# A hybrid decoder step on one core: the last channel mixer's router and row work move ahead of its norm

## The reference

```
def rms_norm(x, g):
    y = x * rsqrt(mean(x * x, axis=-1) + EPS)
    return y * g

hn = rms_norm(h, norm_ffn_g[1])            # the norm this change is about
logits = hn @ router_w                     # 1024 -> 8
top_v, top_i = top_k(logits, 2)
gates = softmax(top_v)
for e in range(8):
    out += combine[:, e] * ((silu(hn @ w_gate[e]) * (hn @ w_up[e])) @ w_down[e])
y = rms_norm(h + out, final_norm_g)
```

## Time and profile before

| what | us |
|---|---|
| median of the runs | 1647.79 |
| the profiled execution | 1648.3 |
| its span, from the first to the last instruction | 1646.6 |
| last product of w_out ends | 819.96 |
| first product of the experts starts | 854.24 |
| PE busy over the span | 1566.2 (95%) |
| mean granted clock of PE | 0.971 |

### The profile page before, as it was taken

The page is one execution under the profiler, slowest core; times in us unless marked ns, Lnnn a source line. Parts: engine busy times, 40 slices in busy tenths (PEclk is TensorE's granted clock), DMA queues, the critical chain, the costliest instruction groups (busy, mean ns, idle before and its releaser), DMA issues.

```text
span 1646.6 us, 25254 instructions
## 1 busy us (share of the span) xinstructions
PE 1566.2 (95%) x8782; PEld 1387.3 (84%) x8783; DVE 1173.3 (71%) x1497; ACT 1000.4 (61%) x1184; POOL 110.6 (7%) x112
## 2 busy tenths in 40 slices
PE   6989999999999998999969999999999999999993
PEld 5889999899999878999858888888888888888882
DVE  6677437544444477734738989898998989898894
ACT  5663324443433575233437787878888787887772
POOL 3020120000000002111000000000000000010000
PEclk9999999999999999999979999999999999999997
DMA  7434453455445332444449999999999999999994
GB/s 221 133 118 128 136 154 117 127 152 145 146 142 159 116 116 93 136 140 128 141 135 352 359 373 372 374 375 366 374 369 372 379 373 369 368 377 366 373 367 155
DMA packets 223037, 399.08 MB, mean 242 GB/s; under 512 B 12336, under 2 KB 103520, under 8 KB 222960
## 3 DMA queue, kind: packets, MB, share of 16 engines
q1 hardware_dynamic: 215920, 372.84, 64.9%
q0 software_dynamic: 6544, 23.37, 5.2%
q10 hardware_dynamic: 496, 1.84, 0.3%
HBM read 383.84 MB, written 14.16 MB: 242 GB/s over the span
## 4 chain that ended last, share of the span: by engine, by line
PE 72%; DVE 9%; ACT 6%; DMA 6%; issue 6%; ACTq 0%; SPq 0%; DVEq 0%; POOLq 0%; POOL 0%
PE bank L1462 10%; PE bank L1464 10%; PE bank L1463 10%; PE bank L1774 7%; PE bank L1776 7%; PE bank L1775 6%; PE bank L1766 4%; PE bank L1765 4%; PE bank L1767 4%; DMA weights_raw<-in_moe_w_up 3%; DVE weights_low L1348 3%; DMA weights_raw<-in_moe_w_down 2%; PE bank L1608 2%; ACT weights_high L909 2%; ACT weights_high L689 2%
## 5 line engine op out<-in xcount | busy, mean ns | idle before, releaser
L1348 DVE TENSOR_TENSOR weights_low<-weights_raw,weights_high 128x1024 fp32r<-128x1024 f32 x522 | 621.4, 1220 | 76.6 <-ACT weights_high L909 65.3
L909 ACT ACTIVATE weights_high<-weights_raw 128x1024 fp32r<-128x1024 f32 x522 | 548.8, 1060 | 144.4 <-DMA weights_raw<-in_moe_w_up 56.4
L972 DVE TENSOR_TENSOR weights_low<-weights_raw,weights_high 128x1024 fp32r<-128x1024 f32 (+1 forms) x186 | 225.2, 1216 | 297.4 <-ACT weights_high L689 297.3
L689 ACT ACTIVATE weights_high<-weights_raw 128x1024 fp32r<-128x1024 f32 (+1 forms) x186 | 193.4, 1045 | 246.6 <-PE bank L1464 236.3
L1462 PE MATMUL bank<-moving_high,weights_high 128*128 128x320 f32 x944 | 299.7, 317 | 1.0 <-DVE moving_low L1043 1.0
L1463 PE MATMUL bank<-moving_low,weights_high 128*128 128x320 f32 x944 | 295.5, 313 | 0.0
L1464 PE MATMUL bank<-moving_high,weights_low 128*128 128x320 f32 x944 | 295.4, 313 | 0.0
L1774 PE MATMUL bank<-weights_high,expert_in_high 128*128 128x512 f32 (+1 forms) x768 | 290.6, 378 | 1.7 <-DVE weights_low L1348 0.8
L1776 PE MATMUL bank<-weights_high,expert_in_low 128*128 128x512 f32 (+1 forms) x768 | 286.6, 373 | 0.0
L1775 PE MATMUL bank<-weights_low,expert_in_high 128*128 128x512 f32 (+1 forms) x768 | 286.4, 373 | 0.0
L1462 PEld LDWEIGHTS bank<-moving_high,weights_high 128*128 128x128 f32 x944 | 181.3, 192 | 4.6 <-issue 1.9
(11 more groups left out here) (298 smaller groups left out, 1813.9 us busy)
## 6 DMA issues: line engine op xcount, KB each, us to landing
weights_raw<-in_moe_w_gate SPq DMA_DIRECT2D x176, 512.0 KB, 5.5
weights_raw<-in_moe_w_up SPq DMA_DIRECT2D x176, 512.0 KB, 5.7
weights_raw<-in_moe_w_down SPq DMA_DIRECT2D x176, 512.0 KB, 5.3
weights_raw<-in_w_in SPq DMA_DIRECT2D x80, 512.0 KB, 3.6
weights_raw<-in_dense_w_gate SPq DMA_DIRECT2D x22, 512.0 KB, 3.8
weights_raw<-in_dense_w_up SPq DMA_DIRECT2D x22, 512.0 KB, 3.7
weights_raw<-in_w_out SPq DMA_DIRECT2D x16, 512.0 KB, 3.4
weights_raw<-in_dense_w_down SPq DMA_DIRECT2D x16, 512.0 KB, 3.4
```

The source lines that it names most:

```text
L689: fn(whi[:, p % RING, 0:n], raw[:, p % RING, 0:n], ACT.Copy).then_inc(high_done, 1)
L909: fn(whi[:, p % RING, 0:n], raw[:, p % RING, 0:n], ACT.Copy).then_inc(high_done, 1)
L1348: v.tensor_tensor(wlo[:, p % RING, 0:n], raw[:, p % RING, 0:n], whi[:, p % RING, 0:n].bitcast(F), ALU.subtract).then_inc(low_done, 1)
```

## The change

Four things. First, the last norm's eight tiles become h times gain, without the inverse root, and are made by DVE right behind each residual tile (line 1092 of the changed kernel). Router products and the turning to rows work on these tiles, most of them between the chunks of w_out; the two best logits of a token are the same with or without a positive factor. Second, the inverse root enters at the difference of the two best logits before Exp, as a third column beside row number and gate, and, by slot, as the scale of Silu and as a factor of the product with up. Third, the squares' sum, the root, the residual's rows and the first expert's gates come behind the first expert's row numbers, and the second half of the rows goes to memory by a shorter write. Fourth, ranks and counts are fewer products, and pick is one instruction for three.

The core of the diff:

```diff
+        HALF = D // 2
+        pool.wait_ge(y_ready, NT)
+        pool.dma_start(HN[0:TP, 0:HALF].rearrange("(t p) d -> p t d", p=128), hn[:, 0:PAIRS, 0:HALF]).then_inc(hn_first, 16)
+        pool.dma_start(HN[TP:T, 0:HALF], hn[0:64, PAIRS, 0:HALF]).then_inc(hn_first, 16)
+        pool.dma_start(HN[T:T + CAP, 0:HALF], hn[:, 0, 0:HALF]).then_inc(hn_first, 16)
+        pool.dma_start(HN[T:T + CAP, HALF:D], hn[:, 0, 0:HALF]).then_inc(hn_first, 16)
+        pool.wait_ge(hn_first, 64)
+        pool.wait_ge(hn_out, 32)
+        pool.wait_ge(idx_ready, 1)
+        pool.indirect_dma_start(out=xrow[:], out_offset=None, in_=HN,
+                                in_offset=bass.IndirectOffsetOnAxis(ap=idx[:, 0:1], axis=0)).then_inc(xrow_in, 16)
...
+        def normed_rows(hf_):
+
+            for t, (_, sz) in enumerate(TOK):
+                act.wait_ge(hn_psum, NT * hf_ + t + 1)
+                fn(hn[0:sz, t, 512 * hf_:512 * hf_ + 512], bank[4 + t][0:sz, :], ACT.Copy).then_inc(y_ready, 1)
...
+                    if L == LAST and part == 3:
+                        act.wait_ge(pstate_out, 16 * LAYERS)
+                        act.wait_ge(vrow_out, 16 * LAYERS)
+                        for q in s0_out:
+                            act.wait_ge(q, 16 * LAYERS)
+                        normed_rows(0)
...
+        normed_rows(1)
+        act.wait_ge(y_ready, NO)
+        act.dma_start(HN[0:TP, 512:D].rearrange("(t p) d -> p t d", p=128), hn[:, 0:PAIRS, 512:D]).then_inc(hn_out, 16)
+        act.dma_start(HN[TP:T, 512:D], hn[0:64, PAIRS, 512:D]).then_inc(hn_out, 16)
+        split_high(NDENSE + AHEAD - 1, 1)
+        act.wait_ge(stat_psum, 2 * LAYERS)
+        fn(rcol[:], bank[2][:, 0:NT], ACT.Sqrt, bias=eps_t[:], scale=1.0 / D).then_inc(root_ready, 1)
+        nc.scalar.preload_act_table(ACT.Exp)
...
-        fn(g1[:, 0], g1[:, 0], ACT.Exp).then_inc(gap_top, 1)
+        fn(g1[:, 1], g1[:, 1], ACT.Exp).then_inc(gap_top, 1)
...
-                fn(sge[:, j % 2, 0:cols], bank[2 * (j % 2)][:, 0:cols], ACT.Silu).then_inc(gate_emptied, 1)
+                if j == 0:
+                    act.wait_ge(rnow_ready, item + 1)
+                fn(sge[:, j % 2, 0:cols], bank[2 * (j % 2)][:, 0:cols], ACT.Silu, scale=rnow[:, 0:1]).then_inc(
+                    gate_emptied, 1)
...
+                        if L == LAST:
+                            dve.wait_ge(dve_emptied, tile[(L, sec, j)][3])
+                            v.tensor_scalar(xn[:, j, :], h[:, j, :], prm[:, P_FFN + KD * L + j:P_FFN + KD * L + j + 1],
+                                            None, ALU.mult).then_inc(xn_ready, 1)
...
+        add_square(2 * LAYERS - 1, KD - 2)
+        add_square(2 * LAYERS - 1, KD - 1)
...
+        v.tensor_tensor(slot[:], bank[0][:, 0:NT * NE].rearrange("p (t e) -> p t e", e=NE), mk[:], ALU.mult).then_inc(
+            shift_done, 1)
...
+        def gates():
+
+            split_low(NDENSE + AHEAD - 1, 1)
+            dve.wait_ge(root_ready, 2 * LAYERS)
+            link(v.tensor_tensor(g1[:, 0], top[:, :, 1], top[:, :, 0], ALU.subtract))
+            link(v.reciprocal(rcol[:], rcol[:]))
+            v.tensor_tensor(g1[:, 1], g1[:, 0], rcol[:], ALU.mult).then_inc(top_ready, 1)
+            v.tensor_copy(pair[:, :, 2:3], rcol[:].unsqueeze(2))
+            dve.wait_ge(count_psum, 1)
+            v.tensor_copy(fullf[:, 0, 0:NE], bank[1][:, 0:NE]).then_inc(count_read, 1)
+            dve.wait_ge(gap_top, 1)
+            link(v.tensor_scalar(g1[:, 0], g1[:, 1], 1.0, None, ALU.add))
+            link(v.reciprocal(g1[:, 2], g1[:, 0]))
+            link(v.tensor_tensor(g1[:, 3], g1[:, 1], g1[:, 2], ALU.mult))
+            link(v.tensor_tensor(m1[:], m1[:], g1[:, 2].unsqueeze(2).broadcast_to([128, NT, NE]), ALU.mult))
+            link(v.tensor_tensor(m2[:], m2[:], g1[:, 3].unsqueeze(2).broadcast_to([128, NT, NE]), ALU.mult))
+            link(v.tensor_tensor(cmb[:], m1[:], m2[:], ALU.add))
+            v.tensor_copy(pair[:, :, 1:2], cmb[:, :, 0:1]).then_inc(pair_ready, 1)
+            dve.wait_ge(gate_psum, 1)
+            v.tensor_copy(gate[:], bank[DOWN_BANK][:, 1:2])
+            link(v.tensor_copy(rnext[:], bank[DOWN_BANK][:, 2:3]))
...
-            for t, (_, sz) in enumerate(TOK):
-                ins = v.tensor_scalar(pick[0:sz, t], iota[0:sz], cslot[0:sz, t:t + 1], None, ALU.is_equal)
-            ins.then_inc(pick_ready, 1)
+                v.tensor_copy(pair[:, :, 1:2], cmb[:, :, bass.ds(e, 1)])
+            v.tensor_tensor(pair[:, :, 0:1], tok_back[:].unsqueeze(2), slot[:, :, bass.ds(e, 1)], ALU.subtract)
+            v.tensor_tensor(pick[:], iota1[:].unsqueeze(1).broadcast_to([128, NT, CAP]),
+                            slot[:, :, bass.ds(e, 1)].broadcast_to([128, NT, CAP]), ALU.is_equal).then_inc(pick_ready, 1)
...
+        def take_inverse_rms(item):
+
+            dve.wait_ge(idx_ready, item + 1)
+            if not isinstance(item, int) or item:
+                dve.wait_ge(gate_emptied, NG * item)
+            v.tensor_copy(rnow[:], rnext[:]).then_inc(rnow_ready, 1)
...
-                v.tensor_tensor(He[:, c0:c0 + cols], bank[1 + 2 * (j % 2)][:, 0:cols], sge[:, j % 2, 0:cols],
-                                ALU.mult).then_inc(he_ready, 1)
+                if j == 0:
+                    dve.wait_ge(rnow_ready, item + 1)
+                v.scalar_tensor_tensor(out=He[:, c0:c0 + cols], in0=bank[1 + 2 * (j % 2)][:, 0:cols], scalar=rnow[:, 0:1],
+                                       in1=sge[:, j % 2, 0:cols], op0=ALU.mult, op1=ALU.mult).then_inc(he_ready, 1)
...
         choose(0, 0)
         rows_of_slots(0)
-
+        gates()
+        take_inverse_rms(0)
         expert_in_low(0)
...
+        def router_products(ks):
+
+            pe.wait_ge(router_in, 16)
+            for k in ks:
+                pe.wait_ge(xn_ready, KD * (2 * LAYERS - 1) + k + 1)
+                for t, (t0, sz) in enumerate(TOK):
+                    ins = mm(bank[7][0:sz, NE * t:NE * t + NE], xn[:, k, t0:t0 + sz], rw[:, k, :], start=k + t == 0,
+                             stop=k == KD - 1 and t == NT - 1, skip_group_check=True)
+            if KD - 1 in ks:
+                ins.then_inc(logit_psum, 1)
+
+        def normed_rows_turned(hf_):
+
+            pe.wait_ge(xn_ready, KD * (2 * LAYERS - 1) + 4 * hf_ + 4)
+            for t, (t0, sz) in enumerate(TOK):
+                if hf_:
+                    pe.wait_ge(y_ready, t + 1)
+                for k in range(4):
+                    ins = nc.tensor.transpose(bank[4 + t][0:sz, 128 * k:128 * k + 128], xn[:, 4 * hf_ + k, t0:t0 + sz],
+                                              ident[:])
+                ins.then_inc(hn_psum, 1)
...
+                    if L == LAST and part:
+                        router_products((2 * part - 2, 2 * part - 1))
+                    if L == LAST and part == 2:
+                        normed_rows_turned(0)
...
+        router_products((KD - 2, KD - 1))
+        normed_rows_turned(1)
         pe.wait_ge(chosen_ready, 1)
+        mm(bank[0][:, 0:NT * NE], upper[:], mk[:].rearrange("p t e -> p (t e)"), start=True, stop=False,
+           skip_group_check=True)
+        for q in range(NT - 1):
+            ins = mm(bank[0][:, NE * (q + 1):NT * NE].rearrange("p (t e) -> p t e", e=NE), ones[:],
+                     mk[:, q:q + 1, :].broadcast_to([128, NT - 1 - q, NE]), start=False, stop=q == NT - 2,
+                     skip_group_check=True)
+        ins.then_inc(rank_psum, 1)
...
+        def first_gates_of_slots():
+
+            pe.wait_ge(pair_ready, 1)
+            pe.wait_ge(idx_ready, 1)
+            for t, (_, sz) in enumerate(TOK):
+                ins = mm(bank[DOWN_BANK][:, 1:3], pick[0:sz, t, :], pair[0:sz, t, 1:3], start=t == 0, stop=t == NT - 1)
+            ins.then_inc(gate_psum, 1)
...
         rows_of_slots(0, 0)
+        pe.wait_ge(summed, KD * 2 * LAYERS)
+        for t, (t0, sz) in enumerate(TOK):
+            if sz < 128:
+                mm(bank[2][:, t:t + 1], ssum[:, 0:128], ones[:, 0:1], start=True, stop=True)
+            ins = mm(bank[2][0:sz, t:t + 1], ssum[:, t0:t0 + sz], ones[:, 0:1], start=True, stop=True)
+        ins.then_inc(stat_psum, 1)
+        for n, (t, hf_) in enumerate(OUTS):
+            t0, sz = TOK[t]
+            if n >= 3:
+                pe.wait_ge(sum_done, n - 2)
+            for k in range(4):
+                ins = nc.tensor.transpose(bank[ROW_BANK[n % 3]][0:sz, 128 * k:128 * k + 128],
+                                          h[:, 4 * hf_ + k, t0:t0 + sz], ident[:])
+            ins.then_inc(sum_psum, 1)
+        first_gates_of_slots()
         expert_rows_turned(0)
```

133 lines of the change are left out of this document (41 added, 92 removed).

## The result

The changed kernel takes 1638.27 us in the median of 5 runs (1635.7 to 1643.58), the kernel before, beside it on the same chip, 1649.31 (1644.64 to 1650.39): a ratio of 0.9926, 95% interval 0.9902 to 0.9949. Predicted were 1638.7 us. The profiled span is 1636.5 us instead of 1646.6.

A forecast was written before the change was run, and what follows sets the result against it. PE was taken to bound w_out and the expert stage, with a 34.28 us serial chain between. Terms a to i sum to 25.19 us, 9.1 less, giving 1638.7 us; range 1633 to 1645.

The forecast's parts named there:

- a: In w_out: four channel tiles of router products and twelve turns put on a full PE, +4.70 us.
- b to e: After w_out, in order: remaining router products +3.28, logits to mask +1.90, ranks, slot and pick +2.20, row numbers +0.95 us.
- f to i: In order: squares' sum through Exp +6.60, DVE's gates +1.50, PE's first gates +1.53, expert's turn to first product +2.53 us.
- The thin place: Before the experts: second-half write and first gather finish ahead of the gates with only a microsecond to spare.
- Rival 2: Before the experts: write and gather end last, gain only 2.6 to 5.4 us, time 1645.2 or 1642.4; chance 0.10.
- The expert stage runs at PE's pace: Expert stage: PE waits for weights only 9 times, 4.6 us in 700, so its end moves with its first product.
- rival 3: Expert stage: weights set the pace, and 1.8 MB of residual rows delay them by 4.9 us, 1643.6; chance 0.07.
- Rival 1: Start of the experts: clock already up, 3.8 us more gained, 1634.9; chance 0.15.
- Rival 4: Expert loop: longer Silu uses up the slack, PE waits at 48 products, 24.5 us lost, 1663; chance 0.05.
- Rival 5: ACT before Exp: table load longer behind a busy ACT, up to 2.41 us, middle 1.2, 1639.9; chance 0.06.

The follow-up runs named there:

- router behind w_out: Changed kernel with all router products and turns to rows put behind w_out instead of between its chunks; 1643.40 us, ratio 0.9972 to the kernel before.
- the second run: The changed kernel run again without any edit, to see how far time and trace repeat; 1636.82 us, ratio 0.9927 to the kernel before.
- Exp first: Changed kernel with the gate's Exp moved ahead of the six copies of the residual's rows; 1636.98 us, ratio 0.9927 to the kernel before.
- With fewer products: Changed kernel leaving out 8 of the 132 down products of each expert, all weights still loaded; 1638.40 us, ratio 0.9940 to the kernel before.
- idle turns: Changed kernel with 16 idle identity turns on PE ahead of the first gates (eight when combined with Exp first); alone 1634.76 us, ratio 0.9911.
- the weights are cut: Changed kernel without half the bytes of each expert's down weights: alone 1637.86 us, 0.9928; with Exp first and eight idle turns 1630.45 us, 0.9877.
- the run with 828.48: The traced run of the changed kernel with the gate's Exp ahead of the six residual copies; median 1636.98 us, ratio 0.9927.

## Why the prediction was right, point by point

**The sum.** It said 25.19 us for the stretch with a, and 9.1 us less; measured are 4.40 + 19.08 = 23.48, and 10.80 less at the first product. The span gained 10.1, because the rest was 0.70 longer, and that rest varies by 3.5 us between two runs of the same kernel. The medians gained 11.0, since the kernel before had 1649.31 us beside the changed one and not the 1647.79 that the forecast started from. Agreement with the median within 0.5 us is thus in part luck.

**a, work put into w_out.** 4.70 expected. The products between the chunks take 1.47 us for each 12, the turns 1.53: 4.47. That w_out's end moved by 4.40 proves less, since it lies between 823.2 and 828.5 in kernels that are equal up to there. What this step missed is why the place pays: the same products cost 4.3 us more behind w_out, where the clock was at 0.50, and the first half's write starts later there (router behind w_out).

**b to e.** b 2.81 (824.36 to 827.17) for 3.28: a router pass takes 2.98 / 24 = 0.124 us in the mean, and starts beside w_out's last. c 1.89 for 1.90. d 1.78 for 2.20: pick takes 0.55 (0.6 taken, bounds 0.3 and 1.1). e 0.92 for 0.95, at full clock as assumed; in the second run 1.52, the other end that the forecast's own range held. There the clock fell near 827.3 while PE was busy (1.00 of the microsecond before it), so the reason given for full clock, that PE has only short gaps, did not decide it: this term was right by luck.

**f to i.** f 6.15 for 6.60, by the way that was forecast: ACT is busy from the root to Exp (0.26, 1.28, 3.46 and 0.20 us in 832.78 to 837.91, neighbours overlapping a little), and Exp ahead of the copies took 2.51 us off the stretch. The copies took 3.46 for 3.3; the squares' sum took 0.98 (831.76 to 832.74) for 1.3. g 1.54 for 1.50, h 1.46 for 1.53 at half clock, i 2.53 for 2.53.

**The gather.** It lands at 838.2, the gates end at 840.98: 2.8 us to spare, one was forecast. The write landed after 3.0 us, not 5.9 (that row is the last of three writes issued one behind the other), and the gather after 4.6, not 9.2 or more. "The thin place" is real: with Exp first it is last by 1.09 us. Rival 2 did not happen in the changed kernel.

**"The expert stage runs at PE's pace".** This step failed as a reason, not in the number. Few waits of PE do not say that the weights have room: they say that the weights are not slower. With fewer products PE waited for weights instead, and the distance stayed. Both floors lie near 95.3 us, which is the premise of rival 3 and that of the forecast at once. The price that rival 3 put on it, 4.9 us for the residual's rows, was not paid: the transfer engines were idle (0.00) from 845 to 849, behind the last of these rows, and nothing shows weights held up by them. That the forecast held because both limits start over with the first product is my reading; no run shows it.

**Rival 1** did not happen in the changed kernel (0.50 in the window at 843), but Exp first and the idle turns show it is to be had; a gain in the time is clear of the noise only where the weights are cut, with Exp first and idle turns together. **Rival 4** is out: Silu is longer by 89 ns (93 forecast, from a row that is a copy with such a scale and not a Silu), PE's waits stay (5.4 us in 11 against 4.6 in 9), and the time is the same without the column. **Rival 5** is out: the load starts 0.02 us behind the root, takes 1.28, and the first copy begins at 834.36, 0.02 behind its end. So the drain of 1.38 us that the Trainium skill (ScalarE: Activation LUTs, What ACT_TABLE_LOAD costs) adds to each switch does not show in this trace either.

**The chances.** The six of them add to 1.00 already, and the share for what was not foreseen, 0.01, comes on top of that; nothing here hangs on it.

**What brought the gain.** Taken back one at a time: router and first half's rows between the chunks are worth 5.1 to 7.6 us of time and 6.2 in the trace, the residual's rows behind the row numbers 6.1 to 7.1 and 2.90. These cannot be added, and the smaller ranks and pick were not tried alone.

**Open.** Why w_out's end varies: in the run with 828.48 the clock was 0.93 from 200 to 300 us, in that with 824.36 it was 0.97, but what decides it is not known. And whether Exp first with idle turns beats the changed kernel: 0.9921 and 0.9926 can't be told apart.

## What to carry to other kernels

Work that a serial stretch needs can be worth putting between full products ahead of it even if it seems to cost the same there: here it ran at a granted clock of 1.00 with half of it between the chunks, and mostly at 0.50 with all of it behind them, and a write that hangs on it started earlier. What nobody waits for belongs behind the address that a gather needs. An engine that is busy all the time is not proven to be the limit: take work from it, and bytes from what feeds it, each alone and then with the gain in question; if neither alone moves the time, two limits may be equal and hide each other's gains, and taking both away at once would show it.
